# Start addresses of the split weights and the split features in a two-model fp32 kernel, and three scratch rows in a shared buffer

## The chip, the core and the metric

The kernel runs on one core of a Trainium2 chip. The metric is the device time of one execution in microseconds: 1168.79 us, the median of three runs (1168.72 to 1170.77). All times below come from these runs or from one profiled execution.

## The reference

Two blocks work one after the other on 256 tokens of 1024 features, in fp32. The first has two layers: an RWKV-7 time mix and a SwiGLU feed-forward, then attention and another SwiGLU feed-forward. The second has an mLSTM beside a forgetting attention, a cross-attention on 256 memory tokens, and a feed-forward with squared ReLU. Nearly all of the work is in products with large weight matrices:

```python
r, k, v = jnp.einsum('nbtc,ncd->nbtd', jnp.stack([xr, xk, xv]), w_rkv)
def swiglu_ffn(x, w_in, w_down):                       # width 2816, twice
    gate, up = jnp.split(x @ w_in, 2, axis=-1)
    return (jax.nn.silu(gate) * up) @ w_down
qkv = (x @ w_qkv)                                      # moba_attention
z = h @ w_in[l]                                        # mLSTM, attention, gates
flf = jax.nn.log_sigmoid(fx_f + fx_b_f[l])             # forget keys' gates
cT = jnp.cumsum(lf, axis=1)
u = jax.nn.relu(rmsnorm(x, ln2[l]) @ w_ff1[l])         # width 4096
x = x + (u * u) @ w_ff2[l]
```

## The kernel before

**Slabs of weights.** Every large weight matrix is cut into slabs of 128 partitions by 2048 fp32 numbers (1 MB), in the order in which they are used. "Wide" slabs hold 1024 input features and 256 outputs, "tall" ones 256 input features and all 1024 outputs. SyncE's queue transfers each slab into one of three slots of `w_raw` (`load`, line 559). ScalarE rounds it to the reduced format fp32r into a slot of `w_hi` (`hi`, line 597), VectorE subtracts and writes the rest into `w_lo` (`lo`, line 1389). Each has three slots (lines 173 to 175). SyncE reloads a slot of `w_raw` when its low part is done; ScalarE overwrites a slot of `w_hi` when TensorE has signalled `slab_done` for the slab three back.

**Three products for one.** The features are split in the same way: `x_hi` and `x_lo` (lines 264 and 265), `mix_hi` and `mix_lo` (177, 178), `rx_hi` and `rx_lo` in the first projections (210, 211), `hid_hi` and `hid_lo` in the feed-forwards. Each product is then made of three fp32r matmuls in `three` (line 2123; its three matmuls are lines 2125, 2126 and 2127): high by high, high by low, low by high. Each matmul loads its stationary operand into the array (a load of weights, PEld in the trace) and streams the other. In `wide_fm` and `wide_as_ready` the weights are stationary and 256 columns of features are streamed; in `wide_tm` the features are stationary and 256 columns of weights are streamed; in `tall_unit` the features are stationary and 512 columns of weights are streamed. Within a tile, all these operands start at whole multiples of 512 bytes from the tile's start. The gates (`gates`, line 2687) are the exception: their stationary operand has 36 columns and starts 144 bytes further for each of the eight k, at the start of `mix_lo`'s fifth row (multiple of 64), and `x_hi` and `x_lo` are streamed.

**Order.** Each engine has its own instruction stream, and semaphores tie them. TensorE goes through the slabs in order; the waits of the feed-forwards and attentions are placed so that its stream seldom stops.

**Addresses.** `sb` allocates SBUF tensors one behind the other, each rounded up to 32 bytes; tensors in an inner `ExitStack` reuse the room of the one before. What follows from that, as bytes in a partition:

| tile | start | modulo 64 |
|---|---|---|
| w_raw | 16512 | 0 |
| w_hi, w_lo | 41088, 65664 | 0, 0 |
| mix_hi, mix_lo | 98432, 106624 | 0, 0 |
| x_hi, x_lo | 118176, 126368 | 32, 32 |
| rx_hi, rx_lo | 175904, 184096 | 32, 32 |
| hid_hi, hid_lo | 182400, 186496 | 0, 0 |
| fx_k | 194688 | 0 |
| zf, za, ones_t, gi | 221312, 222336, 223360, 224384 | 0 |

**Scratch rows.** In the last stages `zf`, `za` and `ones_t` (line 305) are rows of 256 numbers on 12 partitions for the forget gates: VectorE sets `ones_t` to one (line 1926), then `zf`, `za` take the gates' logits and their log-sigmoid, and a scan with `ones_t` signals `gate_rows` (line 1957). ScalarE waits for `gate_rows` (line 1181), then takes ml_v and ml_o, and only then writes the forget attention's queries and keys, `fx_q` and `fx_k` (line 1195).

Of the kernel before, what the change touches and what calls it, by code (L numbers as in the profile page):

```python
# [8 lines left out]
F32R = mybir.dt.float32r  # L9
# [4 lines left out]
P = 128  # L14
T = 256
TT = T // P
C = 1024
KT = C // P
HD = 64
NEG = -1.0e30  # L20
SLAB = 2048
RAW = 3
WS = 3
# [126 lines left out]
    return ap.unsqueeze(2).broadcast_to([ap.shape[0], ap.shape[1], n])  # L150


LORA_B = GLORA - P
GB = 3 * LORA_B
RS = 44


def build(nc, d, out, upto=99):
# [4 lines left out]
    with ExitStack() as ctx:  # L163
        def sb(name, shape, dt=F32, where=None):
            return (where or ctx).enter_context(nc.sbuf_tensor(name, shape, dt))
# [5 lines left out]


        w_raw = sb("w_raw", [P, RAW, SLAB])
        w_hi = sb("w_hi", [P, WS, SLAB], F32R)
        w_lo = sb("w_lo", [P, WS, SLAB], F32R)
        x_tm = sb("x_tm", [P, TT, C])
        mix_hi = sb("mix_hi", [P, KT, T], F32R)
        mix_lo = sb("mix_lo", [P, KT, T], F32R)
# [17 lines left out]
        with ExitStack() as a_rw:  # L196
# [52 lines left out]
            g2, g2b = (sw[:, n:n + 2, :].rearrange("p a b -> p (a b)") for n in (0, 2))  # L249
            sig_g, sig_g2 = sa_m[:, 0, :], sa_m[0:LORA_B, 1, :]  # L250
            y_last_sq = cum[:, :, :].rearrange("p a (b c) -> p (a b) c", c=HD)
# [9 lines left out]


        a_m = ctx.enter_context(ExitStack())
        x_hi = sb("x_hi", [P, KT, T], F32R, a_m)
        x_lo = sb("x_lo", [P, KT, T], F32R, a_m)
        xn = sb("xn", [P, TT, C], where=a_m)
        x_fm = sb("x_fm", [P, KT, T], where=a_m)
        gain = sb("gain", [P, 2, C], where=a_m)
# [26 lines left out]
        with ExitStack() as a:  # L295
# [4 lines left out]
            fx_k = sb("fx_k", [P, 4, T], where=a)  # L300
# [1 line left out]
            se_s = sb("se_s", [P, 4, 3 * P], where=a)  # L302
            se_p = sb("se_p", [P, 4, 3 * P], where=a)
            bias = sb("bias", [P, 4, 3 * P], where=a)
            zf, za, ones_t, gi = (sb(n, [12, T], where=a) for n in ("zf", "za", "ones_t", "gi"))
            gst = sb("gst", [HD, T], where=a)
            tc = sb("tc", [P, TT, HD], where=a)
            em = sb("em", [P, 8], where=a)
# [233 lines left out]
        def _(sp):  # L542
            def load_g(g):
                at = slice(256 * g, 256 * g + 256)
                sp.dma_start(g2, d["g2"][0:P, at]).then_inc(gate_lora_loaded, 16)
                for n in range(3):
                    sp.dma_start(g2b[LORA_B * n:LORA_B * n + LORA_B], d["g2"][P:GLORA, at]).then_inc(gate_lora_loaded, 16)
                if g:
# [45 lines left out]
        def _(act):  # L594
# [248 lines left out]
            nc.scalar.activation(sig_g, ps[:, 5, 0:T], ACT.Sigmoid)  # L843
            nc.scalar.activation(sig_g2, ps[0:LORA_B, 5, T:2 * T], ACT.Sigmoid).then_inc(lora1_out, 1)
            take_rates(3)
# [16 lines left out]
            for g in range(4):  # L862
                for slot in range(SLOTS):
# [12 lines left out]
                    elif g == 0 and slot == 5:  # L876
                        nc.scalar.copy(sig_hi[:, :], sig_g)
                        nc.scalar.copy(sig_b[2 * LORA_B:GB, :], sig_g2)
                        nc.scalar.copy(sig_b[0:LORA_B, :], sig_g2).then_inc(sig_hi_done, 1)
                    if g < 3:  # L880
# [2063 lines left out]
```

## Time and profile before

| | |
|---|---|
| median of three runs | 1168.79 us |
| the profiled execution's span | 1168.6 us |
| TensorE matmuls, busy | 1141.0 us (98%), 10550 |
| loads of weights, busy | 1042.4 us (89%) |
| VectorE, ScalarE, GpSimd busy | 752.2, 623.9, 119.5 us |
| DMA | 187.3 MB, 160 GB/s on average |
| mean granted clock of TensorE | 0.998 |

The profiled execution has a span of 1168.6 us, 0.2 us under the median. PE is TensorE's matmuls and PEld its loads, which overlap them. A matmul's duration includes the way through the array, which overlaps the next one, so that the pace of a series is read from start to start. A group of instructions is named by its line, engine, operation and tiles, output first; the two inputs are written in an order of the program's names, not by role. The chain of work that ended last follows back from the last instruction, at each step to what released it.

### The profile page before, as it was taken

The page shows a single profiled execution, that of the slowest core. Times are in us where ns is not written, and L with a number is a line of the kernel's source. Part 1 is how long each engine was busy: PE and PEld are TensorE (multiplying, and loading weights), DVE is VectorE, ACT ScalarE, POOL GpSimd, SP SyncE. Part 2 cuts the span into 40 slices and gives each one's busy share as a digit, 9 for nine tenths or more (in the row PEclk, how much of TensorE's full clock was granted, in tenths as well). Part 3 has the DMA queues.
Part 4 walks back from the last instruction along what each step waited for, and adds up shares of the span by engine and source line. Part 5 has one row for each costly group of instructions (what it writes and reads, how often), then busy time and mean ns, then how long its engine had stood idle before and what let it go on. Part 6 is the DMA issues. An engine that isn't in the chain of part 4 may idle for free.

```text
span 1168.6 us, 24785 instructions
## 1 busy us (share of the span) xinstructions
PE 1141.0 (98%) x10550; PEld 1042.4 (89%) x10550; DVE 752.2 (64%) x1087; ACT 623.9 (53%) x916; POOL 119.5 (10%) x97
## 2 busy tenths in 40 slices
PE   7999999999999999999999999999999999999997
PEld 7798877789999989988999999899998898999996
DVE  7888886375554467897645445898587555555554
ACT  8974654454433446565634433675566564544443
POOL 0032263401100000220010000011000000000000
PEclk9999999999999999999999999999999999999999
DMA  8631111145554644434555447455434443655550
GB/s 302 226 108 48 55 57 56 61 163 195 195 195 157 244 180 174 151 109 145 180 217 188 179 172 252 147 178 197 164 129 148 158 144 126 217 188 178 211 179 36
DMA packets 29804, 187.30 MB, mean 160 GB/s; under 512 B 3472, under 2 KB 5648, under 8 KB 8592
## 3 DMA queue, kind: packets, MB, share of 16 engines
q1 hardware_dynamic: 27072, 177.21, 42.0%
q10 hardware_dynamic: 2640, 8.75, 2.3%
q8 instruction: 72, 1.18, 0.4%
q14 instruction: 20, 0.16, 0.0%
HBM read 184.90 MB, written 1.05 MB: 159 GB/s over the span
## 4 chain that ended last, share of the span: by engine, by line
PE 87%; DVE 6%; ACT 4%; issue 2%; DMA 0%; ACTq 0%; DVEq 0%; SPq 0%
PE ps L2125 25%; PE ps L2126 24%; PE ps L2127 24%; PE ps L2458 1%; PE ps L2453 1%; PE ps L2599 1%; PE ps L2262 1%; ACT mixed L639 1%; PE ps L2455 1%; DVE w_lo L1396 1%; PE ps L2347 1%; PE ps L2395 1%; PE ps L2846 1%; PE ps L2854 1%; ACT w_hi L745 1%
## 5 line engine op out<-in xcount | busy, mean ns | idle before, releaser
L1400 DVE TENSOR_TENSOR w_lo<-w_raw,w_hi 128x2048 fp32r<-128x2048 f32 x149 | 346.7, 2343 | 125.3 <-ACT w_hi L610 124.6
L2125 PE MATMUL ps<-x_hi,w_hi 128*128 128x256 f32 x1344 | 378.7, 282 | 4.3 <-DVE x_lo L1689 1.5
L2126 PE MATMUL ps<-x_lo,w_hi 128*128 128x256 f32 x1344 | 375.4, 279 | 0.0
L2127 PE MATMUL ps<-x_hi,w_lo 128*128 128x256 f32 x1344 | 375.2, 279 | 0.0
L610 ACT CAST w_hi<-w_raw 128x2048 fp32r<-128x2048 f32 x147 | 280.1, 1907 | 147.6 <-PE ps L2127 147.2
L2125 PEld LDWEIGHTS ps<-x_hi,w_hi 128*128 128x128 f32 x1344 | 252.8, 188 | 11.1 <-issue 4.7
L2126 PEld LDWEIGHTS ps<-x_lo,w_hi 128*128 128x128 f32 x1344 | 252.9, 188 | 1.3
L2127 PEld LDWEIGHTS ps<-x_hi,w_lo 128*128 128x128 f32 x1344 | 252.9, 188 | 0.0
L2125 PE MATMUL ps<-w_hi,hid_hi 128*128 128x512 f32 x304 | 118.8, 391 | 0.1
L2126 PE MATMUL ps<-w_lo,hid_hi 128*128 128x512 f32 x304 | 118.8, 391 | 0.0
L2127 PE MATMUL ps<-w_hi,hid_lo 128*128 128x512 f32 x304 | 118.4, 389 | 0.0
L1788 DVE TENSOR_TENSOR hid<-act_f,ps 128x512 f32<-128x512 f32 x22 | 15.1, 688 | 126.8 <-PE ps L2127 126.8
L1045 ACT ACTIVATE act_f<-ps 128x512 f32<-128x512 f32 x38 | 22.7, 597 | 123.7 <-PE ps L2127 123.7
L2125 PE MATMUL ps<-w_hi,mix_hi 128*128 128x512 f32 (+1 forms) x192 | 73.1, 380 | 0.3 <-DVE mix_lo L1498 0.3
L2127 PE MATMUL ps<-w_hi,mix_lo 128*128 128x512 f32 (+1 forms) x192 | 68.2, 355 | 0.0
L2126 PE MATMUL ps<-w_lo,mix_hi 128*128 128x512 f32 (+1 forms) x192 | 68.0, 354 | 0.0
L2127 PEld LDWEIGHTS ps<-w_hi,hid_lo 128*128 128x128 f32 x304 | 57.1, 188 | 12.2
L2125 PEld LDWEIGHTS ps<-w_hi,hid_hi 128*128 128x128 f32 x304 | 57.1, 188 | 11.4 <-DVE hid_lo L1794 0.5
L2126 PEld LDWEIGHTS ps<-w_lo,hid_hi 128*128 128x128 f32 x304 | 57.1, 188 | 10.5
L2125 PE MATMUL ps<-w_hi,x_hi 128*128 128x256 f32 x224 | 63.1, 282 | 0.0
L2126 PE MATMUL ps<-w_lo,x_hi 128*128 128x256 f32 x224 | 63.0, 281 | 0.0
L2127 PE MATMUL ps<-w_hi,x_lo 128*128 128x256 f32 x224 | 63.0, 281 | 0.0
(419 smaller groups left out, 1782.3 us busy)
## 6 DMA issues: line engine op xcount, KB each, us to landing
w_raw<-in_weights SPq DMA_DIRECT2D x163, 1024.0 KB, 4.9
xt<-in_xT SPq DMA_DIRECT2D x2, 512.0 KB, 5.4
w_raw<-in_weights SPq DMA_DIRECT2D x2, 512.0 KB, 6.2
x_tm<-in_x SPq DMA_DIRECT2D x1, 1024.0 KB, 5.4
gain<-in_mix_g ACTq DMA_DIRECT2D x2, 512.0 KB, 5.1
gain<-in_mix_b ACTq DMA_DIRECT2D x2, 512.0 KB, 6.8
gain<-in_ffn_g ACTq DMA_DIRECT2D x2, 512.0 KB, 7.3
gain<-in_ffn_b ACTq DMA_DIRECT2D x2, 512.0 KB, 9.3
```

What stands on the lines that cost most here:

```text
L610: nc.scalar.copy(w_hi[:, i % WS, :], w_raw[:, i % RAW, :]).then_inc(hi_done, 1)
L639: nc.scalar.activation(mixed[:, q % 2, k, :], xt[:, k, :], ACT.Copy, scale=less_mu[:, at:at + 1]).then_inc(scaled_ready, 1)
L745: ins = nc.scalar.copy(w_hi[:, i % WS, at], w_raw[:, i % RAW, at])
L1045: nc.scalar.activation(act_f[:, j % 2, :], ps[:, 4 + 2 * (j % 2), :], ACT.Relu if name == "ff2" else ACT.Silu).then_inc(ffn_act, 1)
L1396: ins = V.tensor_tensor(halves_placed(w_lo[:, i % WS, :], m), halves_first(w_raw[:, i % RAW, :], m), halves_placed(w_hi[:, i % WS, :], m). ...
L1400: V.tensor_tensor(w_lo[:, i % WS, :], w_raw[:, i % RAW, :], w_hi[:, i % WS, :].bitcast(F32), ALU.subtract).then_inc(lo_done, 1)
L1788: V.tensor_tensor(hid[:, j % 2, :], act_f[:, j % 2, :], ps[:, 5 + 2 * (j % 2), :], ALU.mult).then_inc(ffn_taken, 1)
L2125: nc.tensor.matmul(out, hi_l, hi_r, start=start, stop=False)
L2126: nc.tensor.matmul(out, hi_l, lo_r, start=False, stop=False)
L2127: return nc.tensor.matmul(out, lo_l, hi_r, start=False, stop=stop)
L2262: last = mm(both[q][:, T * m + c0:T * m + T], src[f, 2 * m + t, :], ar[f, 2 * g + m, t, :, :].rearrange("p s c -> p (s c)")[:, c0:T], star ...
L2347: last = mm(z[half, HD * h:HD * h + HD], dd[half, t, 0, s, :], u_m[half, HD * h:HD * h + HD], start=True, stop=True)
```

## The change

`w_hi` and `w_lo` are allocated with 16 more numbers each and begin 4 numbers (16 bytes) into them. `x_hi` and `x_lo` are allocated with 256 more numbers each and begin 160 and 168 numbers into them. By the allocation the starts become 41104 and 65744 for the weights (16 modulo 64) and 118944 and 128192 for the features (32 and 0 modulo 64). What lies between and behind moves: `mix_hi` and `mix_lo`, by 128 bytes, remain 0 modulo 64, `rx_hi` and `rx_lo`, by 128, remain 32, and all that lies behind `x_lo`, `hid` and `fx_k` included, moves by 2176, which is 0 modulo 64. To make room, `zf`, `za` and `ones_t` no longer have tensors of their own but are the first three rows of `fx_k` on 12 partitions. No instruction, wait or transfer is added or taken away.

```diff
--- before.py
+++ after.py
@@ -150,6 +150,8 @@
     return ap.unsqueeze(2).broadcast_to([ap.shape[0], ap.shape[1], n])
 
 
+X_AT = (160, 168)
+W_AT = 4
 LORA_B = GLORA - P
 GB = 3 * LORA_B
 RS = 44
@@ -171,8 +173,8 @@
 
 
         w_raw = sb("w_raw", [P, RAW, SLAB])
-        w_hi = sb("w_hi", [P, WS, SLAB], F32R)
-        w_lo = sb("w_lo", [P, WS, SLAB], F32R)
+        w_hi, w_lo = (sb(name, [P, WS * SLAB + 16], F32R)[:, W_AT:W_AT + WS * SLAB].rearrange("p (s n) -> p s n", s=WS)
+                      for name in ("w_hi", "w_lo"))
         x_tm = sb("x_tm", [P, TT, C])
         mix_hi = sb("mix_hi", [P, KT, T], F32R)
         mix_lo = sb("mix_lo", [P, KT, T], F32R)
@@ -261,8 +263,8 @@
 
 
         a_m = ctx.enter_context(ExitStack())
-        x_hi = sb("x_hi", [P, KT, T], F32R, a_m)
-        x_lo = sb("x_lo", [P, KT, T], F32R, a_m)
+        x_hi, x_lo = (sb(name, [P, KT * T + 256], F32R, a_m)[:, n:n + KT * T].rearrange("p (k c) -> p k c", k=KT)
+                      for name, n in (("x_hi", X_AT[0]), ("x_lo", X_AT[1])))
         xn = sb("xn", [P, TT, C], where=a_m)
         x_fm = sb("x_fm", [P, KT, T], where=a_m)
         gain = sb("gain", [P, 2, C], where=a_m)
@@ -302,7 +304,8 @@
             se_s = sb("se_s", [P, 4, 3 * P], where=a)
             se_p = sb("se_p", [P, 4, 3 * P], where=a)
             bias = sb("bias", [P, 4, 3 * P], where=a)
-            zf, za, ones_t, gi = (sb(n, [12, T], where=a) for n in ("zf", "za", "ones_t", "gi"))
+            gi = sb("gi", [12, T], where=a)
+            zf, za, ones_t = (fx_k[0:12, n, :] for n in range(3))
             gst = sb("gst", [HD, T], where=a)
             tc = sb("tc", [P, TT, HD], where=a)
             em = sb("em", [P, 8], where=a)
```

## Rows read from the trace of the kernel before

**Rows 1.** The page: busy times, GB/s by slice, chain by line.
```profile
PE 1141.0 (98%) x10550; PEld 1042.4 (89%) x10550; DVE 752.2 (64%) x1087; ACT 623.9 (53%) x916; POOL 119.5 (10%) x97
...
GB/s 302 226 108 48 55 57 56 61 163 195 195 195 157 244 180 174 151 109 145 180 217 188 179 172 252 147 178 197 164 129 148 158 144 126 217 188 178 211 179 36
...
PE ps L2125 25%; PE ps L2126 24%; PE ps L2127 24%; PE ps L2458 1%; PE ps L2453 1%; PE ps L2599 1%; PE ps L2262 1%; ACT mixed L639 1%; PE ps L2455 1%; DVE w_lo L1396 1%; PE ps L2347 1%; PE ps L2395 1%; PE ps L2846 1%; PE ps L2854 1%; ACT w_hi L745 1%
```

**Rows 2.** Windows: busy us of each engine (instructions), PEclk, DMA share, GB/s.
```profile
560.00:720.00 160.00, 159.84 (x1162) 150.85 (x1162) 84.03 (x57) 69.91 (x56) 10.34 (x8) 1.00 0.55 201
1000.00:1160.00 160.00, 159.90 (x1030) 145.28 (x1029) 86.41 (x63) 71.68 (x61) 0.00 (x0) 1.00 0.49 170
```

**Rows 3.** Lines: line, engine, op, tiles, shapes, count | busy us, mean ns | idle.
```profile
L2125 PE MATMUL ps<-x_hi,w_hi 128*128 128x256 f32 x1344 | 378.7, 282 | 4.3 <-DVE x_lo L1689 1.5 <-ACT fx_q L1073 0.7 <-DVE x_lo L1698 0.5
...
L2125 PE MATMUL ps<-w_hi,hid_hi 128*128 128x512 f32 x304 | 118.8, 391 | 0.1
...
L2125 PE MATMUL ps<-w_hi,mix_hi 128*128 128x512 f32 (+1 forms) x192 | 73.1, 380 | 0.3 <-DVE mix_lo L1498 0.3
...
L2125 PE MATMUL ps<-w_hi,x_hi 128*128 128x256 f32 x224 | 63.1, 282 | 0.0
...
L2125 PE MATMUL ps<-mix_hi,w_hi 128*128 128x256 f32 x64 | 18.3, 286 | 0.7 <-DVE mix_lo L1414 0.7
L2125 PE MATMUL ps<-rx_hi,w_hi 128*128 128x256 f32 x64 | 18.1, 283 | 0.0
...
L2125 PE MATMUL ps<-w_hi,mix_hi 128*128 128x512 f32 x128 | 52.4, 409 | 0.3 <-DVE mix_lo L1498 0.3
```

**Rows 4.** Timeline (start us, duration us, instruction): weights in the array, x streamed, last products.
```profile
1012.00 0.28 PE L2127 MATMUL ps<-x_hi,w_lo 128*128 128x256 f32 x1
...
1017.25 0.28 PE L2127 MATMUL ps<-x_hi,w_lo 128*128 128x256 f32 x1
```

**Rows 5.** Timeline: x in the array, weights streamed.
```profile
824.85 0.29 PE L2127 MATMUL ps<-w_hi,x_lo 128*128 128x256 f32 x1
...
831.25 0.28 PE L2127 MATMUL ps<-w_hi,x_lo 128*128 128x256 f32 x1
```

**Rows 6.** Timeline: weights in the array, rx streamed.
```profile
60.14 0.28 PE L2127 MATMUL ps<-rx_hi,w_lo 128*128 128x256 f32 x1
...
65.42 0.28 PE L2127 MATMUL ps<-rx_hi,w_lo 128*128 128x256 f32 x1
```

**Rows 7.** Timeline: weights in the array, mix streamed.
```profile
15.26 0.28 PE L2127 MATMUL ps<-mix_hi,w_lo 128*128 128x256 f32 x1
...
21.74 0.28 PE L2127 MATMUL ps<-mix_hi,w_lo 128*128 128x256 f32 x1
```

**Rows 8.** Timeline: hid in the array, 512 columns of weights streamed.
```profile
735.02 0.39 PE L2127 MATMUL ps<-w_hi,hid_lo 128*128 128x512 f32 x1
...
741.14 0.39 PE L2127 MATMUL ps<-w_hi,hid_lo 128*128 128x512 f32 x1
```

**Rows 9.** Timeline: loads of weights (PEld) beside a product (PE).
```profile
1014.22 0.19 PEld L2126 LDWEIGHTS ps<-x_lo,w_hi 128*128 128x128 f32 x1
...
1014.22 0.28 PE L2125 MATMUL ps<-x_hi,w_hi 128*128 128x256 f32 x1
```

**Rows 10.** Timeline: products of the gates, from the fifth, seventh and eighth k, the end.
```profile
754.50 0.28 PE L2125 MATMUL ps<-x_hi,mix_lo 128*36 128x256 f32 x1
...
755.18 0.28 PE L2125 MATMUL ps<-x_hi,mix_lo 128*36 128x256 f32 x1
...
755.53 0.28 PE L2125 MATMUL ps<-x_hi,mix_lo 128*36 128x256 f32 x1
...
755.89 0.28 PE L2125 MATMUL ps<-x_hi,w_hi 128*128 128x256 f32 x1
```

**Rows 11.** Timeline of ScalarE and VectorE: one slab's cast and subtraction.
```profile
1012.02 1.91 ACT L610 CAST w_hi<-w_raw 128x2048 fp32r<-128x2048 f32 x1 [1.68 <-PE ps L2127]
...
1013.96 2.29 DVE L1400 TENSOR_TENSOR w_lo<-w_raw,w_hi 128x2048 fp32r<-128x2048 f32 x1 [1.30 <-ACT w_hi L610]
```

## Prediction

> **What bounds the kernel now.** I read the page first. TensorE is busy for 98% of the span, and its clock is granted in full, 1.00, in long stretches [rows 1, 2]. The chain of work that ended last lies for 73% on three lines, L2125 to L2127, the three products that every split matmul is made of [rows 1]. DMA moves 160 GB/s on average, against 302 in its first slice [rows 1], so the transfers of weights are not the limit. The reader is to see that only TensorE's pace on three lines can move the time much: 1% of it is worth 853 us (73% of 1168.6) x 1% = 8.5 us.
>
> Then the grouped lines, for how many products of which shape there are, each group once on each of the three lines [rows 3]: 1344 x 3 = 4032 with the weights in the array and 256 columns of x_hi or x_lo streamed; 224 x 3 = 672 with x in the array and 256 columns of weights streamed; 64 x 3 = 192 with rx; 64 x 3 = 192 with mix streamed against weights, and as many the other way round (64 of the 192 w_hi,mix_hi), so 384 with mix at 256 columns; and 304 x 3 = 912 with hid and 128 x 3 = 384 with mix at 512 columns, together 1296. In all 6576.
>
> Then the timeline, for the distance from start to start, because a matmul's own duration contains a tail that overlaps the next. Two rows on the same line, divided by the products between them:
> - weights against x: 1012.00 to 1017.25, 45 products, 116.7 ns [rows 4];
> - x against weights: 824.85 to 831.25, 54 products, 118.5 ns [rows 5];
> - weights against rx: 60.14 to 65.42, 45 products, 117.3 ns [rows 6];
> - weights against mix: 15.26 to 21.74, 54 products, 120.0 ns [rows 7];
> - hid against weights, 512 columns: 735.02 to 741.14, 27 products, 226.7 ns [rows 8].
>
> The last two differ by 106.7 ns for 256 columns more. So 256 columns cost 106.7 ns, which is the full clock, 2.4 GHz, at a column a tick, and each product has a fixed part above its columns: 10.0, 11.8, 10.6, 13.3 and 13.4 ns in the order of the list. This fixed part is all that the change can touch. It comes to 4032 x 10.0 + 672 x 11.8 + 192 x 10.6 + 384 x 13.3 + 1296 x 13.4 = 40.3 + 7.9 + 2.0 + 5.1 + 17.4 = 72.7 us.
>
> **Why it may depend on addresses.** From the allocation, given above, the distance of the two operands (start of the streamed tile minus start of the one that is loaded meanwhile for the next product, modulo 64 bytes) is 32 for the first three of the list and 0 for the last two. Distance 0 has 13.3 and 13.4, distance 32 has 10.0 to 11.8. The same shape of 128x128 against 256 columns shows both values (116.7 and 120.0), at the same clock, so the shape doesn't explain it; each load of weights starts with the product before it [rows 9], so both operands are being read at once. A third look is the products of the gates: x_hi and x_lo streamed as always, but a load of 36 columns that starts 144 bytes further each k. The fifth and sixth k take 0.68 us, 6 products, 113.3 ns [rows 10], a fixed part of 6.6; the seventh takes 0.35 us, 116.7 ns, and the last 0.36 us, 120 ns. Same streams, other starts of the load, three levels with steps of about 3.3 ns. This is the nearest row for a distance that is neither 0 nor 32: by address the fifth k has 32, the sixth 16, the last 48.
>
> **The change part by part.** *Weights at 16, x_hi at 32, x_lo at 0 modulo 64.* No instruction comes or goes. After it every split product has a distance of 16 or of 48: x_hi or rx (still at 32) streamed against weights 16, x_lo or mix (still at 0) 48; weights streamed against x_hi 48, against x_lo, hid or mix 16. No row shows a full load at either distance, so I bound the new fixed part v by the rows: 6.6 ns from below [rows 10] and 13.4 from above [rows 8]. With the same v for all 6576 the fixed parts become 6.576 x v us against 72.7, so the break-even is v = 11.05 ns. Only 853 us of the 912 us that these products take (470.5 + 79.6 + 22.5 + 46.1 + 293.8) lie on the chain, a share of 0.935, so a difference counts 0.935 times. v = 6.6: 43.4, -27.4 us; v = 8.3, halfway between the two best levels: 54.6, -16.9 us; v = 10.0: 65.8, -6.5 us; v = 11.7: 76.9, +4.0 us; v = 13.4: 88.1, +14.4 us. I take 8.3. The reason is that distance 0 is the worst level in each pair of rows, that leaving it for 32 gave 3.3 ns, and that the gates show a level below 10.0, once at a distance of 16; that all pairs take one value is a guess, and I keep both ends.
>
> The Trainium skill (TensorE: Matmul & The Clock Gate, Part 1, "Wait — 56ns, not 53.3ns?") gives a matmul its columns at 2.4 GHz plus about 2.5 ns, with no word on addresses; by it nothing would move and the time would be 1168.8. The trace disagrees with the figure, 10.0 to 13.4 here against 2.5, so I don't follow it beyond a rival.
>
> *Casts.* ScalarE writes w_hi and VectorE reads it and writes w_lo at the new start, 1.91 and 2.29 us a slab. If either became 10% slower, 0.2 us, nothing waits: the cast starts at 1012.02, after 1.68 us of waiting for TensorE to leave the slot, the subtraction runs from 1013.96 to 1016.25, and TensorE comes to that slot only two slabs on, 48 x 116.7 + 24 x 226.7 ns = 11.0 us after 1012 [rows 4, 8, 11]. Cover 6.8 us; cost 0. The transfers into w_raw keep their addresses; a faster TensorE frees slots sooner by at most 0.2 us a slab, against stretches that run at 170 and 201 GB/s [rows 2]. No queue becomes the bound.
>
> *Scratch rows.* zf, za and ones_t lie in the first twelve partitions of fx_k. Their last reader is the scan before gate_rows; ScalarE waits for gate_rows and then takes ml_v and ml_o before it writes fx_k. So no wait is added and nothing is queued behind one; cost 0. Were there a collision, it would be wrong numbers, not time. Tiles behind the weights move by 128 bytes and behind x_lo by 2176, both 0 modulo 64; at 0.
>
> **The sum**: span 1168.6 - 16.9 = 1151.7, and 0.2 outside it as now (median 1168.8), 1151.9.
>
> **The rivals.**
> - *Only the clash at 0 goes.* 16 and 48 behave like 32: v = 10.0 and 1168.8 - 6.5 = 1162.3. For it: at distance 32 three different pairs of tiles lie within 1.8 ns of each other [rows 4 to 6]. Against: the 6.6 of the gates [rows 10]. Chance 0.21.
> - *Nothing moves.* The levels belong to something else than the start (the stage, the tile), 1168.8. For it: rx and x differ by 0.6 ns at the same distance modulo 64. The skill's rule above would give this time too. Chance 0.09.
> - *x loses its good spacing.* 32 is the best distance there is and 16 and 48 lie between it and 0: v = 11.7 gives 1172.8, and v = 13.4, as bad as mix today, 1183.2. It decides from v = 11.05. The place is the 4032 products of weights against x, 1.7 to 3.4 ns each, +6.9 to +13.7 us before the share, against which the 1680 products at distance 0 give back at most 2.8. For it: 16 is nearer to 0 than 32 is, and the gates' last k, at a distance of 48, had 120 ns [rows 10]. Chance 0.26.
> - *The fixed part nearly vanishes*, v under 5, below 1132: no row shows it. Chance 0.04.
>
> **How the numbers follow.** The forecast, v between 6.6 and 9.6, 1141 to 1160, has 0.40. About 0.2% or 2.3 us is what a measurement of this kernel can tell from no change. Faster: 0.40 + 0.21 + 0.04 = 0.65; same 0.09; slower 0.26. The range goes from 1140 to 1177: it leaves out the last rival and the worse half of the third, together about 0.17.
>
> **What would show it right or wrong.** In the timeline of after, 45 products of weights against x should take 45 x 115.0 = 5.18 us instead of 5.25; three products of hid 0.665 instead of 0.68. The counts of all groups, the casts' 1.91 and 2.29 us, the clock of 1.00 and the 73% stay. Shorter distances with the same time would mean that another wait took the gain, to be seen as idle time before L2125. Wrong is the forecast if x_hi's and x_lo's products go apart, one shorter and one longer, since I gave them one v, or if the fixed part rises while all distances are 16 or 48.

## The result and the profile after

The changed kernel takes 1179.48 us (median, 1178.24 to 1179.92) beside 1168.88 for the kernel before: ratio 1.0084, 95% interval 1.0072 to 1.0096. It is slower by about 10.6 us, where 1151.9 was forecast. The experiments below are held against the kernel before as measured beside each of them, 1169.87 to 1170.17 us. The profiled execution's span is 1178.1 us, 9.5 more than before, at the same mean granted clock, 0.998.

From the page of the changed kernel: the busy times, the chain by line, then groups (line, engine, operation, tiles, count | busy us, mean ns of one | idle), to be held against [rows 1, 3]. Lines 2125 to 2127 are 2128 to 2130 here.

```profile
PE 1150.2 (98%) x10550; PEld 1045.8 (89%) x10550; DVE 751.7 (64%) x1087; ACT 623.9 (53%) x916; POOL 119.5 (10%) x97
...
PE ps L2128 25%; PE ps L2130 25%; PE ps L2129 25%; PE ps L2461 1%; PE ps L2456 1%; PE ps L2602 1%; PE ps L2265 1%; PE ps L2458 1%; PE ps L2350 1%; PE ps L2398 1%; PE ps L2849 1%; PE ps L2857 1%; DMA w_raw<-in_weights 1%; ACT mixed L642 1%; ACT w_hi L748 1%
...
L1403 DVE TENSOR_TENSOR w_lo<-w_raw,w_hi 128x2048 fp32r<-128x2048 f32 x149 | 345.8, 2337 | 129.8 <-ACT w_hi L613 129.1
L2128 PE MATMUL ps<-x_hi,w_hi 128*128 128x256 f32 x1344 | 377.4, 281 | 4.3 <-DVE x_lo L1692 1.5
L2130 PE MATMUL ps<-x_hi,w_lo 128*128 128x256 f32 x1344 | 378.8, 282 | 0.0
L2129 PE MATMUL ps<-x_lo,w_hi 128*128 128x256 f32 x1344 | 373.8, 278 | 0.0
...
L2128 PE MATMUL ps<-w_hi,hid_hi 128*128 128x512 f32 x304 | 119.9, 394 | 0.1
```

The other two lines of x in the kernel before, which [rows 3] leaves out:

```profile
L2126 PE MATMUL ps<-x_lo,w_hi 128*128 128x256 f32 x1344 | 375.4, 279 | 0.0
L2127 PE MATMUL ps<-x_hi,w_lo 128*128 128x256 f32 x1344 | 375.2, 279 | 0.0
```

Counts, the other engines' busy times and the idle time ahead of these products are those of before (4.3 and 0.1 us on the two groups, as there), and TensorE's idle time in total is 27.9 us after 27.6. Its busy time is 9.2 us longer, and that is nearly all of the 9.5. So no wait of any size was added; the products take more time. Those of hid have 394 ns where [rows 3] has 391. Of x's three lines, 282, 279 and 279 ns before, the last went up to 282 and the others down to 281 and 278; a duration holds the overlapping tail, so what a product costs is read from start to start.

The timeline of the changed kernel (start us, duration us, instruction) answers to [rows 7, 8, 5, 4] in this order; between the two rows of a pair lie 54, 27, 54 and 45 products.

```profile
16.00 0.28 PE L2130 MATMUL ps<-mix_hi,w_lo 128*128 128x256 f32 x1
...
22.39 0.28 PE L2130 MATMUL ps<-mix_hi,w_lo 128*128 128x256 f32 x1
...
736.50 0.40 PE L2130 MATMUL ps<-w_hi,hid_lo 128*128 128x512 f32 x1
...
742.78 0.40 PE L2130 MATMUL ps<-w_hi,hid_lo 128*128 128x512 f32 x1
...
827.95 0.28 PE L2130 MATMUL ps<-w_hi,x_lo 128*128 128x256 f32 x1
...
834.31 0.28 PE L2130 MATMUL ps<-w_hi,x_lo 128*128 128x256 f32 x1
...
1019.34 0.28 PE L2130 MATMUL ps<-x_hi,w_lo 128*128 128x256 f32 x1
...
1024.64 0.28 PE L2130 MATMUL ps<-x_hi,w_lo 128*128 128x256 f32 x1
```

Start to start that is 118.3 ns for mix (before 120.0), 232.6 for hid (226.7), 117.8 for weights against x in the array (118.5) and 117.8 for x against weights in the array (116.7). The small groups gained and the two large ones lost. The 512-column products, which had the "worst" distance by the prediction, lost most.

The same reading over whole groups, for the kernel before, the changed one, and those of the experiments below, except scratch_only, whose groups are those of before within 1 ns a triple. Each number is the time of a triple (the sum of the mean start-to-start times of its three products, gaps over 1.1 times the median left out); the last rows give the sum over all triples against before, and the span of the profiled execution against 1168.6 us.

| | triples | before | after | w_only | x_only | hid_follows | x_at_0 | x_at_192 | x_at_112 |
|---|---|---|---|---|---|---|---|---|---|
| weights loaded, x streamed | 1344 | 350.5 | 353.5 | 358.0 | 354.0 | 353.4 | 359.5 | 350.0 | 342.0 |
| x loaded, weights streamed | 224 | 354.8 | 353.3 | 360.0 | 353.6 | 353.4 | 359.8 | 348.6 | 359.8 |
| hid, 512 columns | 304 | 683.0 | 698.4 | 698.7 | 685.0 | 690.9 | 683.3 | 680.3 | 683.3 |
| mix, 512 columns | 128 | 685.2 | 698.7 | 698.7 | 685.8 | 693.2 | 685.7 | 685.2 | 685.0 |
| mix 256, rx: us against before | 192 | | -0.3 | -0.7 | +0.2 | -0.5 | 0 | 0 | +0.2 |
| sum, us against before | | | +9.9 | +17.0 | +5.3 | +6.5 | +13.4 | -2.9 | -10.0 |
| span, us against before | | | +9.5 | +14.9 | +3.0 | +4.5 | +11.1 | -1.7 | -8.6 |

For the changed kernel: x +4.1 us (1344 x 3.0 ns) and -0.3 the other way round, hid +4.7, mix at 512 columns +1.7, the rest -0.3. Together +9.9, the whole of the 9.5. In the other columns sum and span differ by up to 2.3 us: a part of the products is not on the chain, and single executions of one kernel differ by 1 to 2 us.

Theories at this point: (A) the pace of an fp32r product follows from the start addresses alone, but not modulo 64 and not in the same way at 256 and 512 columns; (B) the place, the tile or what other engines do at the time decides, and the addresses only shift it; (C) the scratch rows or the features' larger room cost the time.

### The profile page after: what moved, and what is told of

The parts are those of the page before. It is cut to its first block, busy times and chain, and to the rows that moved or that the text cites. A ratio compares the mean times of both kernels' runs of the same rounds, so it can differ in the third digit from the quotient of the medians.

```text
span 1178.1 us, 24785 instructions
## 1 busy us (share of the span) xinstructions
PE 1150.2 (98%) x10550; PEld 1045.8 (89%) x10550; DVE 751.7 (64%) x1087; ACT 623.9 (53%) x916; POOL 119.5 (10%) x97
## 4 chain that ended last, share of the span: by engine, by line
PE 87%; DVE 6%; ACT 4%; issue 1%; DMA 1%; ACTq 0%; SPq 0%; DVEq 0%
PE ps L2128 25%; PE ps L2130 25%; PE ps L2129 25%; PE ps L2461 1%; PE ps L2456 1%; PE ps L2602 1%; PE ps L2265 1%; PE ps L2458 1%; PE ps L2350 1%; PE ps L2398 1%; PE ps L2849 1%; PE ps L2857 1%; DMA w_raw<-in_weights 1%; ACT mixed L642 1%; ACT w_hi L748 1%
## 5 line engine op out<-in xcount | busy, mean ns | idle before, releaser
L1403 DVE TENSOR_TENSOR w_lo<-w_raw,w_hi 128x2048 fp32r<-128x2048 f32 x149 | 345.8, 2337 | 129.8 <-ACT w_hi L613 129.1
L2128 PE MATMUL ps<-x_hi,w_hi 128*128 128x256 f32 x1344 | 377.4, 281 | 4.3 <-DVE x_lo L1692 1.5
L2130 PE MATMUL ps<-x_hi,w_lo 128*128 128x256 f32 x1344 | 378.8, 282 | 0.0
L2129 PE MATMUL ps<-x_lo,w_hi 128*128 128x256 f32 x1344 | 373.8, 278 | 0.0
L613 ACT CAST w_hi<-w_raw 128x2048 fp32r<-128x2048 f32 x147 | 279.9, 1905 | 153.1 <-PE ps L2130 152.6
L2128 PEld LDWEIGHTS ps<-x_hi,w_hi 128*128 128x128 f32 x1344 | 252.3, 188 | 11.2 <-issue 4.7
L2129 PEld LDWEIGHTS ps<-x_lo,w_hi 128*128 128x128 f32 x1344 | 251.6, 187 | 1.4
L2130 PEld LDWEIGHTS ps<-x_hi,w_lo 128*128 128x128 f32 x1344 | 252.3, 188 | 0.0
L2129 PE MATMUL ps<-w_lo,hid_hi 128*128 128x512 f32 x304 | 120.4, 396 | 0.0
L2130 PE MATMUL ps<-w_hi,hid_lo 128*128 128x512 f32 x304 | 120.0, 395 | 0.0
L2128 PE MATMUL ps<-w_hi,hid_hi 128*128 128x512 f32 x304 | 119.9, 394 | 0.1
L2128 PE MATMUL ps<-w_hi,mix_hi 128*128 128x512 f32 (+1 forms) x192 | 73.3, 382 | 0.3 <-DVE mix_lo L1501 0.3
L2130 PEld LDWEIGHTS ps<-w_hi,hid_lo 128*128 128x128 f32 x304 | 57.0, 188 | 13.4
L2129 PE MATMUL ps<-w_lo,mix_hi 128*128 128x512 f32 (+1 forms) x192 | 68.8, 358 | 0.0
L2128 PEld LDWEIGHTS ps<-w_hi,hid_hi 128*128 128x128 f32 x304 | 57.3, 188 | 12.9 <-DVE hid_lo L1797 0.5
L2130 PE MATMUL ps<-w_hi,mix_lo 128*128 128x512 f32 (+1 forms) x192 | 68.6, 357 | 0.0
L2129 PEld LDWEIGHTS ps<-w_lo,hid_hi 128*128 128x128 f32 x304 | 57.2, 188 | 11.7
L2128 PE MATMUL ps<-w_hi,x_hi 128*128 128x256 f32 x224 | 63.0, 281 | 0.0
L2129 PE MATMUL ps<-w_lo,x_hi 128*128 128x256 f32 x224 | 63.0, 281 | 0.0
L2130 PE MATMUL ps<-w_hi,x_lo 128*128 128x256 f32 x224 | 62.5, 279 | 0.0
```

The lines of the kernel that those rows point to most:

```text
L613: nc.scalar.copy(w_hi[:, i % WS, :], w_raw[:, i % RAW, :]).then_inc(hi_done, 1)
L1403: V.tensor_tensor(w_lo[:, i % WS, :], w_raw[:, i % RAW, :], w_hi[:, i % WS, :].bitcast(F32), ALU.subtract).then_inc(lo_done, 1)
L2128: nc.tensor.matmul(out, hi_l, hi_r, start=start, stop=False)
L2129: nc.tensor.matmul(out, hi_l, lo_r, start=False, stop=False)
L2130: return nc.tensor.matmul(out, lo_l, hi_r, start=False, stop=stop)
```

## The experiments

### m1_map: products alone

A kernel of TensorE matmuls only, all other engines idle; it computes nothing of the reference. Series of 24 products, weights at one start, the streamed tile at another (here loaded at 0 and streamed 32 bytes on); then triples with the starts of both kernels, modulo 256.

```python
for j in range(24): mm(ps[0:128, 2, 0:256], A(0, j // 3, 128), B(32, j // 3, 256), start=j == 0, stop=j == 23)
```

> Not the kernel's computation: it copies the input x to its output and beside that only runs series of 24 (or 48) matmuls of rounded copies of x, one load of 128 columns and 256 or 512 streamed columns each, with the other engines idle; each series has its own start addresses of the loaded and of the streamed tile. It measures the disputed cost by itself. Theory R (only the distance between the streamed and the loaded start counts): at distance 0 about 120.0 ns per product of 256 columns and 226.7 of 512, as in the kernel before; at distance 32 about 117; series that share a distance but not the starts agree within 0.5 ns; and the 512-column series at distance 16 has some 233 ns, as in the changed kernel. Theory S (the start of an operand past a multiple of 64 bytes counts by itself): series with both starts at 0, 16, 32 or 64 differ although all have distance 0, the ones at 16 by 5 ns or more at 512 columns. A third possibility: nothing depends on starts when VectorE and ScalarE are idle, all 256-column series alike within 0.5 ns; then the pace comes from the other engines' accesses.

Timeline of m1_map (start us, duration us, line, count). Lines 54 to 69 are the streamed starts 0, 16, ... 240 bytes at 256 columns, 70 to 85 the same at 512, all with the loaded tile at 0. Line 92 has it at 112 and streams from 0; 101 has both tiles at 16, 102 the loaded one at 16 and the streamed one at 32. The time between two neighbouring starts, divided by 24, gives the pace.

```profile
24.04 3.04 PE L54 MATMUL ps<-streamed_t,loaded_t 128*128 128x256 f32 x24
26.92 3.02 PE L55 MATMUL ps<-streamed_t,loaded_t 128*128 128x256 f32 x24
29.78 2.96 PE L56 MATMUL ps<-streamed_t,loaded_t 128*128 128x256 f32 x24
32.58 3.00 PE L57 MATMUL ps<-streamed_t,loaded_t 128*128 128x256 f32 x24
...
44.01 2.88 PE L61 MATMUL ps<-streamed_t,loaded_t 128*128 128x256 f32 x24
46.73 3.00 PE L62 MATMUL ps<-streamed_t,loaded_t 128*128 128x256 f32 x24
...
69.34 5.65 PE L70 MATMUL ps<-streamed_t,loaded_t 128*128 128x512 f32 x24
74.83 5.72 PE L71 MATMUL ps<-streamed_t,loaded_t 128*128 128x512 f32 x24
80.38 5.77 PE L72 MATMUL ps<-streamed_t,loaded_t 128*128 128x512 f32 x24
85.99 5.76 PE L73 MATMUL ps<-streamed_t,loaded_t 128*128 128x512 f32 x24
...
175.34 3.04 PE L92 MATMUL ps<-streamed_t,loaded_t 128*128 128x256 f32 x24
178.22 3.00 PE L93 MATMUL ps<-streamed_t,loaded_t 128*128 128x256 f32 x24
...
201.08 5.69 PE L101 MATMUL ps<-streamed_t,loaded_t 128*128 128x512 f32 x24
206.61 5.64 PE L102 MATMUL ps<-streamed_t,loaded_t 128*128 128x512 f32 x24
```

Mean start-to-start times within the series, first three left out (ns), with the loaded tile at 0:

| streamed start | 0 | 16 | 32 | 48 | 64 | 80 | 96 | 112 | 128 | 144 | 160 | 176 | 192 | 208 | 224 | 240 |
|---|---|---|---|---|---|---|---|---|---|---|---|---|---|---|---|---|
| 256 columns | 120.0 | 118.7 | 116.7 | 118.4 | 118.0 | 120.0 | 120.1 | 113.4 | 118.4 | 118.7 | 117.3 | 119.3 | 113.4 | 119.5 | 118.5 | 117.2 |
| 512 columns | 228.3 | 231.7 | 233.3 | 233.4 | 229.2 | 231.2 | 233.7 | 231.4 | 232.4 | 233.2 | 233.9 | 233.0 | 233.4 | 234.7 | 233.4 | 226.7 |

At 256 columns 0 is indeed among the slowest, 120.0 ns, but 64, which is the same modulo 64, has 118.0, 192 has 113.4 and 96 has 120.1 where 32 has 116.7. At 512 columns 0 is next to the fastest (median 227), and 16 to 48 cost 3 to 5 ns more. The triples at the kernels' addresses gave, a product: x streamed 116.8 before and 117.7 after, weights streamed against x 118.4 and 117.8, 512 columns 227.2 and 232.8, mix at 256 columns 120.0 and 118.5. These are the paces of the real kernels, 116.7 to 117.8, 118.5 to 117.8, 226.7 to 232.6 and 120.0 to 118.3, with no other engine at work. Theory B falls. Plain fp32 products of 256 columns kept one pace, 215.8 ns a record with two records each, at the four streamed starts tried (0, 16, 32, 64). A load of 32 columns had other levels than one of 128 (117.8, 113.7, 117.4 at 0, 16, 32 bytes).

The distance alone is not enough either. With the loaded tile at 32, 64 or 96 a distance had the pace of the table at 256 columns within 0.1 ns, but with it 16 past a multiple of 32 it had another: both tiles at 16 took 118.3 ns (256 columns) and 230.0 (512) where both at 0 took 120.0 and 228.3, 16 with 32 took 117.4 and 228.4 where 0 with 16 took 118.7 and 231.7, and 112 with 0 (distance 144) took 120.4 where 0 with 144 took 118.7. Of the two theories in the expectation, R thus fails there, and S's 5 ns at 512 columns was 1.8. At distance 192 the start made no such difference: m2_map below has 113.4 and 113.8 from 16 and 48. The changed kernel's weights start at 144 and 208 modulo 256, both 16 past a multiple of 32, so this table is not made for its products against x.

### w_only, x_only, hid_follows: the parts of the change

w_only changes only the weights' tiles (first part of the diff); as these grow by 64 bytes each, all that lies behind them, x and hid included, moves by 128 bytes as well. x_only moves only the features and has the shared scratch rows. hid_follows is the changed kernel with hid and mix moved along with the weights, x at the very same addresses:

```diff
-X_AT = (160, 168)
+X_AT = (128, 136)
 ...
-        mix_hi = sb("mix_hi", [P, KT, T], F32R)
-        mix_lo = sb("mix_lo", [P, KT, T], F32R)
+        mix_hi, mix_lo = (sb(name, [P, KT * T + 16], F32R)[:, W_AT:W_AT + KT * T].rearrange("p (k c) -> p k c", k=KT)
+                          for name in ("mix_hi", "mix_lo"))
 ...
-            hid_hi = sb("hid_hi", [P, 2, 512], F32R, a)
-            hid_lo = sb("hid_lo", [P, 2, 512], F32R, a)
+            hid_hi, hid_lo = (sb(name, [P, 1024 + 16], F32R, a)[:, W_AT:W_AT + 1024].rearrange("p (s n) -> p s n", s=2)
+                              for name in ("hid_hi", "hid_lo"))
```

> The kernel before with only the weights moved by 16 bytes (w_hi, w_lo at 16 modulo 64); x_hi and x_lo stay at 32. If the loss comes with the weights' start, the products with 512 streamed columns take about 233 ns instead of 227 and the time is 1175 to 1180 us. If it comes from the place of x, these stay at 227 and the time is 1168.9. R and S agree here for the 512-column products; for weights against x (all three distances now 16) R expects what the two x_hi products of the changed kernel have, 119.0 on average, +2.3 ns, 4032 of them, so 9 us more on top of 6, about 1183; S expects 117.8, the changed kernel's mean, about 1179.

> The changed kernel with the weights back at a multiple of 64; x_hi at 32 (as before modulo 64), x_lo at 0, scratch rows shared. Both theories: 512-column products at 227 ns, so at least 6 us less than the changed kernel, 1173 or under. R: x_hi against weights keeps distance 32 and its 117; x_lo against weights gets distance 0 and 120: a third of 4032 products by 3.3 ns, +4 us, 1173. S: no product starts at 16, 1168.9.

> The changed kernel with hid_hi, hid_lo, mix_hi and mix_lo moved by 16 bytes too, so that they are again at distance 0 from the weights; x_hi and x_lo at exactly the changed kernel's addresses. R: the 1296 products with 512 columns go back from 233 to 227 ns, 6 to 7 us less, about 1173, the x products unchanged. S: nothing comes back, 1179 to 1180.

| | median us | ratio to before | 95% interval |
|---|---|---|---|
| w_only | 1186.05 | 1.0137 | 1.0120 to 1.0154 |
| x_only | 1174.57 | 1.0041 | 1.0026 to 1.0055 |
| hid_follows | 1176.40 | 1.0059 | 1.0042 to 1.0076 |

Both parts lose by themselves, and the parts do not add up (1.37% and 0.41% against 0.84% together), since the pace hangs on both starts: w_only's x stands 144, 144 and 80 bytes past its weights, which is neither kernel's spacing. Changing the weights alone costs hid the same 15.7 ns a triple as the whole change (15.4), and x_only leaves hid within 2 ns of before, so the 6.4 us of the 512-column products come from the weights' part of the change. That part is not 16 bytes alone: against hid the weights went from a distance of 0 to 144 and 208, since the larger tiles moved hid and w_lo too. Giving hid and mix the weights' offset brought half of hid's loss back and two fifths of mix's. In hid_follows' timeline, 27 products of hid lie between

```profile
732.91 0.39 PE L2130 MATMUL ps<-w_hi,hid_lo 128*128 128x512 f32 x1
...
739.13 0.39 PE L2130 MATMUL ps<-w_hi,hid_lo 128*128 128x512 f32 x1
```

230.4 ns each, between 226.7 and 232.6. Why it is half is not shown. Two readings fit. In the first the allocation is the reason: w_hi grew by 64 bytes, so w_lo now begins 64 bytes past w_hi modulo 256, and hid_lo past hid_hi as well, and the distances of a triple, each product's streamed tile against its own loaded one, are 0, 64 and 192, not three times 0 (m1_map: 228.3, 229.2 and 233.4, mean 230.3). But the prediction's pairs, the streamed tile against the one loaded meanwhile for the next product [rows 9], have three times 0 here. In the second reading the starts themselves are the reason, 144 and 208, 16 past a multiple of 32: both tiles at 16 took 230.0 ns in m1_map. No run separates the two. (mix came to 128, 192 and 64, so it tests neither.)

### m2_map: which distance counts

Products alone again (nothing of the reference): starts of the loaded tile 0, 64, 128 and 192 with eight streamed starts each, other column counts, and triples of mixed distances.

```python
for j in range(48): mm(ps[:, 2, 0:256], A((0, 0, 0)[j % 3], j // 6, 128, ...), B((192, 0, 192)[j % 3], j // 6, 256, ...), start=j == 0, stop=j == 47)  # distance 192 and 0 in turn
```

> Again not the kernel's computation but series of matmuls of rounded copies of the input, other engines idle; x is copied to the output. The first series repeat eight distances (steps of 32) from four starts of the loaded tile (0, 64, 128, 192) with 256 columns. M: all series of one distance modulo 256 agree within 0.5 ns whatever the start, 113.35 at 192, 120.0 at 0 and 96, and so also at 448 (192 more 256). R: the values repeat every 64 bytes. With 512 columns, distance 0 has 227 from every start and distance 64 some 229; with 384 and 128 columns I expect 160.0 + 10 to 13 and, since then the load is as long as the stream, no less than 106.7 ns for 128. Of the triples, weights against x at 192 should take 113.35 on average and the other way round 118; a triple that changes its distance between 192 and 0 shows whether its pace is the mean of the two, (2 x 113.35 + 120) / 3 = 115.6.

By the distance modulo 256 (streamed minus loaded) the four loaded starts agree: 0 gives 119.7 to 120.0 ns, 32 117.8, 96 119.6 to 120.1, 128 118.6 to 118.7, 192 113.3 to 113.4, 224 118.2. Two pairs stand out: 192 loaded with 0 streamed (distance 64) has 113.3 instead of 117.8, and 128 loaded with 32 streamed (160) has 118.6 instead of 117.3 to 117.4. 128 columns take 111.6 to 111.9 ns at every distance, and 384 columns 173.3 to 174.7, a little over the 170 to 173 expected. Equal starts at 512 columns have a median of 227 ns from each of the four starts. Four things did not fit a table of distances. 448 bytes, 192 and 256 more, had 117.8 ns, not the expected 113.4. Distance 240 at 512 columns, the fastest in m1_map with 226.7, had 236.6 to 236.7 from three of the loaded starts and 233.3 from the fourth. Distance 112 had 115.3 ns here and 113.4 in m1_map, 32 had 117.8 and 116.7. And a triple of distances 192, 0, 192 ran at 117.8 a product, where the mean of its parts would be 115.6; with 192 three times it ran at 113.3. So the pace is no sum over single pairs, and it seems to depend on what ran before. The same holds for mix at 256 columns in the changed kernel: distances 112, 112 and 48, for which the single series would give 115.1 on average, and 118.4 measured.

### x_at_192, x_at_0, scratch_only: two distances that are equal modulo 64

The kernel before with the scratch rows shared, and x_hi and x_lo moved by a gap; weights, hid and mix stay. With 40 numbers x begins 192 bytes past the weights modulo 256, with 56 numbers 0; both are 0 modulo 64. scratch_only is the scratch rows alone.

```diff
+        sb("x_gap", [P, 40], where=a_m)
         x_hi = sb("x_hi", [P, KT, T], F32R, a_m)
         x_lo = sb("x_lo", [P, KT, T], F32R, a_m)
+        sb("x_end", [P, 24], where=a_m)
```

> The kernel before with the shared scratch rows, weights untouched, and x_hi and x_lo moved so that both start 192 bytes behind the weights modulo 256 (0 modulo 64). Theory M (the pace is a function of the distance modulo 256 and of the number of streamed columns, as the first map shows it): 113.35 ns instead of 116.8 for the 4032 products of weights against x, 13.9 us less, and 118.0 instead of 118.4 for the 672 the other way round, 0.3 less; 512-column products unchanged; ratio 0.988. Theory R (only modulo 64 counts): distance 0, 120 ns, 13 us more, ratio 1.012.

> The same, but x_hi and x_lo start 0 bytes behind the weights modulo 256; modulo 64 it is the same place as in the run at 192. Both M and R expect 120.0 ns for the 4032 and for the 672 products, 13 + 1 us more than before, ratio 1.012. If this and the run at 192 give the same time, R holds and M falls.

> The kernel before with the three scratch rows in fx_k and nothing else. All theories: no change, ratio within 0.998 to 1.002. Over 1.002 would put a part of the loss on the scratch rows.

| | median us | ratio to before | 95% interval |
|---|---|---|---|
| x_at_192 | 1169.24 | 0.9989 | 0.9979 to 0.9999 |
| x_at_0 | 1181.08 | 1.0088 | 1.0071 to 1.0104 |
| scratch_only | 1170.64 | 1.0003 | 0.9994 to 1.0013 |

The scratch rows cost nothing that can be measured, and x_at_192, with 256 bytes more room around the features, lost nothing: theory C falls, since the groups' paces also leave nothing for the 2048 bytes of the changed kernel to cost. The two x distances, equal modulo 64, are 1.0% of the time apart: the distance modulo 64, on which the prediction rested, is not the quantity. x_at_0 behaved as the series had said, 119.9 ns a product. x_at_192 did not: it has both paces, here 45 products each time in its timeline, in a stretch right behind twelve products of the attention and in the squared-ReLU feed-forward.

```profile
499.97 0.28 PE L2130 MATMUL ps<-x_hi,w_lo 128*128 128x256 f32 x1
...
505.08 0.28 PE L2130 MATMUL ps<-x_hi,w_lo 128*128 128x256 f32 x1
...
1009.99 0.28 PE L2130 MATMUL ps<-x_hi,w_lo 128*128 128x256 f32 x1
...
1015.28 0.28 PE L2130 MATMUL ps<-x_hi,w_lo 128*128 128x256 f32 x1
```

That is 113.6 and 117.6 ns, at the same addresses, shapes and clock. Taken 24 at a time, the products with x streamed make 166 groups. The 100 that follow hid's 512-column products ran at 117.7 to 117.8 without exception; of the other 66, 42 ran at 113.3 to 114.6, 19 at 117 or more, and 5 between. The last neighbour alone doesn't choose: a stretch at 477 us, behind twelve products of the attention as the one at 500 us, had 117.8.

### m3_cycle: what ran before

Products alone, once more nothing of the reference: each series of 48 products of 256 columns stands behind 24 of 512 columns with equal starts, or behind something else.

```python
for j in range(24): mm(ps[:, 0, 0:512], A(0, j // 3, 128), B(0, j // 3, 512), start=j == 0, stop=j == 23)
for j in range(48): mm(ps[:, 3, 0:256], A(0, j // 6, 128), B(192, j // 6, 256), start=j == 0, stop=j == 47)
```

> A kernel of matmuls alone; it computes nothing of the reference (its output is a copy of the input). Each series of 48 products of 256 columns stands right behind 24 products of 512 columns whose two operands have equal starts, as in the feed-forwards, for streamed starts 0 to 240 bytes past the loaded one in steps of 16; then the same at 192 bytes with something between the two series: a wait that holds already, one product of 32 columns, one of 128, one plain fp32 product; and at 192 bytes behind wide products of other distances. Theory 'the history decides': at 192 bytes 117.8 ns right behind the 512-column products and 113.3 ns behind a short product or a plain one; some other start keeps 113.3 to 116.6 ns behind the wide ones. Theory 'the distance decides alone': 113.3 ns at 192 bytes in every surrounding, 116.7 at 32, 120.0 at 0, and then the 117.8 ns of the real kernel's feed-forwards must have a cause outside TensorE.

Timeline of m3_cycle. Lines 69 and 79 are 112 and 192 bytes behind 512 columns of distance 0; 87 is 192 behind 256 columns of distance 0; 111 is 192 behind 512 columns of distance 16. Lines 115 and 121 are 512 columns of distance 240, the one behind 256 columns of distance 192, the other behind 256 of distance 0. The series of 48 lasts until the next row's start.

```profile
107.66 5.64 PE L69 MATMUL ps<-streamed_t,loaded_t 128*128 128x256 f32 x48
113.14 5.63 PE L70 MATMUL ps<-streamed_t,loaded_t 128*128 128x512 f32 x24
...
163.21 5.82 PE L79 MATMUL ps<-streamed_t,loaded_t 128*128 128x256 f32 x48
168.87 5.60 PE L80 MATMUL ps<-streamed_t,loaded_t 128*128 128x512 f32 x24
...
205.14 5.62 PE L87 MATMUL ps<-streamed_t,loaded_t 128*128 128x256 f32 x48
210.60 3.02 PE L88 MATMUL ps<-streamed_t,loaded_t 128*128 128x256 f32 x24
...
309.09 5.61 PE L111 MATMUL ps<-streamed_t,loaded_t 128*128 128x256 f32 x48
314.54 5.76 PE L112 MATMUL ps<-streamed_t,loaded_t 128*128 128x512 f32 x24
...
328.30 11.50 PE L115 MATMUL ps<-streamed_t,loaded_t 128*128 128x512 f32 x48
339.63 2.90 PE L116 MATMUL ps<-streamed_t,loaded_t 128*128 128x256 f32 x24
...
369.97 11.05 PE L121 MATMUL ps<-streamed_t,loaded_t 128*128 128x512 f32 x48
380.86 3.03 PE L122 MATMUL ps<-streamed_t,loaded_t 128*128 128x256 f32 x24
```

At 192 bytes the same 48 products take 5.66 us (117.8 ns) behind 512 columns of distance 0, but 5.46 behind 256 columns and 5.45 behind 512 columns of distance 16 (113.3 to 113.4 without the first three, L87 in the same output bank as L79). Behind 512 columns of distance 32 it was 113.3 too, behind those of 64 and 240 it was 117.8. So one distance has two paces, and what ran before chooses. The distance of the series before does not say which: behind 48 products of distance 240 that ran at 236.4 ns, 192 had 113.4, and behind 24 of the same distance that ran at 233.3 it had 117.8. The 512-column products have such paces themselves: distance 240 took 236.4 ns behind distance 192 (line 115) and 226.7 behind distance 0 (line 121), and 64 took 228.9 and 233.3. With both tiles at 0, 512 columns kept a median of 227 in every series of m3_cycle. Nothing put between the series made it leave the longer one: a wait that held already, a product of 32 columns, one of 128, a plain fp32 product each left 117.8. This goes against the part of the expectation by which a short product would do. Distance 112 ran at 114.1 ns behind 512 columns, the best of the sixteen; 32 had 116.7, 144 had 116.7, 0 had 120.0. So theory A holds for the addresses together with the order in which the products run, not for the addresses alone.

### x_at_112: the start of the fastest series, in the real kernel

The kernel before with the scratch rows shared and x 112 bytes past the weights modulo 256.

```diff
-        x_hi = sb("x_hi", [P, KT, T], F32R, a_m)
-        x_lo = sb("x_lo", [P, KT, T], F32R, a_m)
+        sb("x_gap", [P, 16], where=a_m)
+        x_hi, x_lo = (sb(name, [P, KT * T + 64], F32R, a_m)[:, 4:4 + KT * T].rearrange("p (k c) -> p k c", k=KT)
+                      for name in ("x_hi", "x_lo"))
+        sb("x_end", [P, 48], where=a_m)
 ...
```

> The kernel before with the three scratch rows shared and one thing moved: x_hi and x_lo begin 112 bytes past the split weights modulo 256 (before 32); weights, hidden and mixed features stay where they were, 0 from one another. The series of matmuls alone gave, for 256 columns right behind 512-column products of distance 0, 114.1 ns at 112 bytes against 116.7 at 32, and 116.7 for the other direction (144), which stands at 118.3 in the kernel before. Theory 'start distance modulo 256 and what ran before, nothing else': 4032 feature-major x products go from 116.8 to 114.1 (-10.9 us) and 672 token-major ones from 118.3 to 116.7 (-1.1), 512-column products stay at 227 to 228: about 1158 us against 1170, ratio 0.990; if the x products settle at the 115.3 that the second series gave at 112 without wide ones ahead, -6 us, 1163. Theory 'the real kernel sits in the slower of two states wherever the series does' (as it did at 192 bytes, 117.8 where 113.3 was hoped for): no gain, 1167 to 1172.

1161.77 us (1160.52 to 1164.04), ratio 0.9929, interval 0.9915 to 0.9943: faster than both kernels, by 0.7% and 1.5%. Groups of x_at_112 (line, engine, operation, tiles, count | busy us, mean ns of one | idle us and what ended it):

```profile
L2128 PE MATMUL ps<-x_hi,w_hi 128*128 128x256 f32 x1344 | 374.2, 278 | 4.8 <-DVE x_lo L1692 1.5 <-DVE w_lo L1403 1.5 <-DVE x_lo L1701 0.5
L2129 PE MATMUL ps<-x_lo,w_hi 128*128 128x256 f32 x1344 | 370.8, 276 | 0.0
L2130 PE MATMUL ps<-x_hi,w_lo 128*128 128x256 f32 x1344 | 370.6, 276 | 0.0
```

Its timeline, 45 products between the two rows, 114.0 ns each:

```profile
1015.85 0.28 PE L2130 MATMUL ps<-x_hi,w_lo 128*128 128x256 f32 x1
...
1020.98 0.28 PE L2130 MATMUL ps<-x_hi,w_lo 128*128 128x256 f32 x1
```

The products of x streamed gave 11.4 us, as the series had said (114.0 against 114.1 ns). The other direction did not follow the series from which the forecast was taken: 119.9 ns where 116.7 was hoped for, +1.1 us instead of -1.1. That series had the loaded tile at 0 and the streamed one at 144; in the kernel x is loaded from a start 16 past a multiple of 32, and the series of m1_map that has this too, loaded at 112 and streamed at 0, ran at 120.4 (line 92). And the line shows three waits for w_lo, 1.5 us in all, so TensorE now comes up to VectorE's subtraction; its idle time in total grew by only 0.4 us over before. The direction accounts for 2.2 of the 4 us between 1158 and 1162; the waits and the spread of single executions are of the size of the rest.

## Why the prediction was wrong

**What bounds the kernel: right.** Only TensorE's pace on three lines moved the time, with waits, clock and counts unchanged. All seven groups together give +9.9 us against 9.5 of span; the share of 0.935 taken for the chain was near enough.

**That start addresses set the fixed part: right.** m1_map showed it with the other engines idle. The row behind it, two paces for one shape at one clock [rows 4, 7], was a sound reading. The Trainium skill's figure (TensorE: Matmul & The Clock Gate, Part 1, "Wait — 56ns, not 53.3ns?"), columns plus about 2.5 ns with no word on addresses, holds for no fp32r series here: the fixed part was 6.6 to 16.7 ns at 256 columns and 13.3 to 23.4 at 512. By it nothing would have moved, and x_at_0 and x_at_112 are 1.7% apart.

**The step that failed: "distance 0 is the worst level in each pair of rows", and with it one value v for all 6576 products.** The prediction put the 1296 products of 512 columns [rows 8] beside the 384 of mix at 256 [rows 7], because both had 13.3 to 13.4 ns at distance 0, and expected both to gain. No row compared 512 columns at two distances. Nor did the gates bear it out: their seventh k, 0 modulo 64 by its address, had 116.7 ns, less than the last k's 120 at 48 [rows 10]. At 512 columns 0 is one of the best distances and 144 and 208, where the change puts them, are among the worst (233.2 and 234.7): these products had the most to lose. Counted as a gain of 5.1 ns each (6.6 us), they lost 6.4 us, which is 13 us of the forecast's error of 27.6 (12.2 at the share of 0.935). v = 8.3 for the 4032 products of x was the other part: 115.0 forecast, 117.8 measured, 11.3 us. The small groups, forecast at 115.0 and measured at 117.8 to 119.5, add nearly 4 us, and with the share of 0.935 all of it comes to 26.4; the last 1.2 us are within the spread of single executions.

**The step beneath it: the distance taken modulo 64.** Modulo 64 the change gives 16 or 48 everywhere. Modulo 256 w_lo begins 64 bytes past w_hi, because the tile of w_hi grew by 64, and x's triple has distances 16, 48 and 208, hid's 144, 208 and 144 (each product's streamed tile against its own loaded one). x_at_192 and x_at_0 settled it: equal modulo 64, 11.8 us apart. The allocation was there to be read; the modulus was chosen with two values in hand. The distance modulo 256 is not the whole quantity either: for x's triple the single series give 118.9 on average and the kernel had 117.8, which is as much as the 1.0 ns that x lost. What reproduced the kernel were only the series with its own starts, 117.7.

**The gates' rows [rows 10] were no lower bound.** They were read as a low level at 16 modulo 64. A load of 32 columns has its own levels, as m1_map showed, so the 113.3 ns did not carry over to loads of 128, though that level exists there too, at 112 and 192 bytes. That no series of 128x128 products went below 6.6 is luck: these rows could not show it.

**The sign named as "wrong" was the right one.** The prediction would be wrong if x_hi's and x_lo's products went apart: they did, by start to start 117.5, 115.5 and 120.5 on L2128, L2129 and L2130. x_lo, at its own distance, gained, and the others lost.

**The rivals.** "x loses its good spacing" had the right sign and its place, at +1.0 ns a product instead of 1.7 to 3.4; that the measured time lies between its two values is luck. But it gave the 512-column products to the gaining side, and without their 6.4 us it would have ended at +3.5. So the slow outcome came from two losses, and the larger one no rival named. The casts (1905 and 2337 ns, as before) and the scratch rows cost nothing, as said.

## What to carry to other kernels

Where TensorE's products of split fp32r operands are the chain, the starts of the loaded and the streamed tile are worth 1 to 2% of the time, here 1161.8 to 1186.1 us. Read the pace from start to start by group and column count. Before a start is chosen, measure the candidates in a series of products alone, with both starts as in the kernel, not their distance alone, and in the order and with the neighbours that the kernel has. A level seen at one column count says nothing of another, and padding one tile of a pair moves its partner and all that lies behind.

## What the runs showed of the hardware

The fixed part of an fp32r product of 128x128 by 256 columns, its pace less 106.7 ns, ranged from 6.6 to 13.7 ns over starts that are multiples of 16 bytes and reached 16.7 with the streamed tile 4 bytes on (123.4 ns, m1_map). By 512 columns it ranged from 13.3 to 23.4 (226.6 to 236.7 ns). By 128 columns all four distances tried took 111.6 to 111.9, hardly less than the fastest series of 256 columns. Plain fp32 kept one pace at four starts.

A distance of 192 bytes has two paces at 256 columns, 113.3 and 117.8 ns, at the same addresses, and one of 240 bytes has 226.7, 233.3 and 236.4 at 512 columns. Which one holds depends on the series before, and the longer one of 192 survived a wait, two short products and a plain one. A triple of mixed distances (192, 0, 192) runs at 117.8, not at the mean. A loaded tile that starts 16 bytes past a multiple of 32 had other paces at most distances tried (both tiles at 16: 230.0 ns by 512 columns, both at 0: 228.3), the same one at 192.

That the distance repeats every 256 bytes rests on the four loaded starts of m2_map, with two exceptions, and the one series a whole 256 bytes further on, 448, had the other pace of 192. What in the chip all this comes from stays open: no run separates the reads of the load from those of the stream, nor the start of a tile from what ran before it.
